# Seven column blocks of one projection multiplied with seven block products in place of eight, in a trunk layer in fp32

## The chip, the cores and the metric

The kernel runs on one core of one Trainium2 chip. The metric is the device time of one execution in microseconds (us). Everything that the text touches is fp32. The engines are named as the profile names them: PE is the matrix engine (TensorE), PEld its weight loads, DVE is VectorE, ACT is ScalarE, POOL is GpSimd, SP is the engine that issues most of the weight loads; SPq, ACTq and so on are their instruction queues.

## The reference, cut to what matters

The layer takes 384 tokens (128 of context and 256 latent ones) of width 1024. The change is in one product, `h @ w_in`, and only in some of its columns: the output gate of the linear attention (`g_out`, 512 columns) and the two branch gates (`gate_br_conv` and `gate_br_gla`, 1024 columns each).

```
h = rmsnorm(x, norm1_w) * (1 + sc1) + sh1
(u_in, gate_b, gate_c, q, k, v, g_out, lr_f, lr_b,
 gate_br_conv, gate_br_gla) = jnp.split(h @ w_in, points, axis=-1)
y_conv = gate_b * conv3_rows(gate_c * u_in, conv_w, conv_b, rows, row_len)
y_gla, s_f, s_b = gla_mixer(q, k, v, g_out, lr_f, lr_b, ...)      # ends in  o * silu(g_out)
merged = (sigmoid(gate_br_conv) * (y_conv @ w_br_conv)
          + sigmoid(gate_br_gla) * (y_gla @ w_br_gla))
x = x + g1 * (merged @ w_out)
h2 = rmsnorm(x, norm2_w) * (1 + sc2) + sh2
x = x + g2 * moe(h2, ...)                                          # 64 experts, top 8, and a shared one
```

The modulation rows `sh1 ... g2` are `silu(cond) @ w_mod + b_mod`, with `w_mod` of 1024 x 6144.

## The kernel before, in words

The normalised input lies transposed in `hT`: 128 partitions, 8 blocks of features (k), 384 tokens. A column tile of the projection is 128 columns of `w_in`: `project_part` (L1904) runs 8 matmuls for it, one for each k, each with 128 x 128 weights and 384 moving columns (L1910), into one of the 8 PSUM banks. The profile shows each fp32 matmul as two records. In the names of the code "u", "gc", "gb", "k", "q", "v", "go", "gbc" and "gbg" are the pieces of `w_in`: "go" is `g_out` (4 column tiles), "gbc" and "gbg" are the branch gates (8 tiles each).

**Units.** Weights come in units of 1 MB: two column tiles of `w_in` (so "go" has units 0 and 1, "gbg" units 0 to 3), or one k of a third of `w_mod` ("mod"). The units stand in one written order, `plan_units` (L103), and go through a ring of 5 places. SP loads a unit into the place of the unit five earlier in the order (L1561), in order, and waits before it until that older unit has been used: for a unit of `w_in` until PE has finished its last tile, for a "mod" unit until DVE has added it. Around the change the order is v0, v1, mod 1.4, go0, mod 1.5, go1, mod 1.6, gbc0, mod 1.7, gbc1, gbc2, gbc3, mod 2.0, mod 2.1, gbg0, mod 2.2, mod 2.3, gbg1, mod 2.4, mod 2.5, gbg2, mod 2.6, mod 2.7, gbg3, and then the weights of the branch projections. ("mod 2.3" is k = 3 of the last third of `w_mod`.)

**Modulation.** DVE multiplies each "mod" unit by the activated condition and adds it, in `add_modulation` (L463: two scalar_tensor_tensor of 128 x 2048, one for each condition). PE then sums the result over the partitions in `sum_modulation` (L1900), which waits until all 8 units of that third have been added: `sum_modulation(1)` stands behind the attention's transposes (L2014), `sum_modulation(2)` between gbg tiles 5 and 6.

**Order of the work.** It is written out by hand for each engine. PE: u, gc, gb, k, q, v, then the four "go" tiles, eight groups of three transposes ("kt", L2014), `sum_modulation(1)`, the attention with gbc tiles 0 to 3 between its pieces, gbc 4 and 5, the transposes of the attention's output ("oT", L2025), gbc 6 and 7, gbg 0 to 5, `sum_modulation(2)`, gbg 6 and 7, the branch projections ("mc", "mg", L2082), the output projection (L2096), routing and experts. A job of PE takes a bank in the turn that `plan_jobs` and `bank_of` set and waits (`start`) until the job before in that bank has been drained. ACT drains the gate tiles with Silu (L1754) or Sigmoid (L1762). POOL has nothing to do between its constants at the start and the expert stage. DVE works through its own list: after gate factors and the sums of `mod 1`, the attention's masks and states, the output's norm, and then mod 2.1 to 2.7 in one row.

## Time and profile before

| | us |
|---|---|
| median of 3 runs (955.33 to 955.88) | 955.38 |
| the profiled execution, whole | 957.51 |
| its span, first to last instruction | 955.8 |
| PE busy (95% of the span) | 910.9 |
| DVE busy (45%) | 426.2 |
| ACT busy (20%) | 187.8 |
| POOL busy (10%) | 94.7 |
| POOL: 34 indirect stores of expert rows (L597), 30 indirect loads (L591), mean of one | 1.01, 1.06 |

The mean granted clock of TensorE was 0.992. The profiled execution is 2.1 us longer than the median. The busy share of PE is an average: the projection (up to 288 us from the span's start), the branch and output projections (to 385 us) and the expert stage (to about 907 us) each have a limit of their own, and so a stage is read by itself. In the page's row of 40 slices the DMA engines are at 3 to 7 tenths in most slices up to 400 us and at 9 in all behind it.

### The profile page before, as it was taken

To read this page: it belongs to the slowest core of one execution; us is meant where nothing else is said; L and a number is where in the kernel's file an instruction comes from. 1 tells how busy PE (TensorE), PEld (TensorE's weight loads), DVE (VectorE), ACT (ScalarE), POOL (GpSimd) and SP (SyncE) were. 2 spreads that over 40 slices of the span, in tenths; PEclk is the share of its full clock that TensorE was granted. 3 is DMA by queue.
4 is the path that set the end of the run, shared out by engine and by line. 5 is a ranking of instruction groups with operands and counts; after the bars stand their busy time and mean duration, and the time that the engine had idled before them with its cause. 6 is when DMAs were issued, how large, how long until landed. Compare 5 with 4: busy or idle time off the path is not lost.

```text
span 955.8 us, 13246 instructions
## 1 busy us (share of the span) xinstructions
PE 910.9 (95%) x4997; PEld 487.7 (51%) x4997; DVE 426.2 (45%) x770; ACT 187.8 (20%) x309; POOL 94.7 (10%) x198
## 2 busy tenths in 40 slices
PE   5999999999999999999999999989999989899995
PEld 2455567676555687544444444434445453454432
DVE  4129966534762346463333333323233323323267
ACT  3150601212100013112212212111111211211111
POOL 2000000000000000202112111111111201111100
PEclk9999999999999999999999999999999999999998
DMA  9998453625677356799999999999999999999995
GB/s 344 355 404 327 132 201 142 229 89 177 237 292 269 125 245 240 279 395 374 420 419 420 420 420 420 420 421 421 419 421 419 421 423 418 423 420 420 420 418 220
DMA packets 85034, 322.04 MB, mean 337 GB/s; under 512 B 10084, under 2 KB 38936, under 8 KB 56040
## 3 DMA queue, kind: packets, MB, share of 16 engines
q1 hardware_dynamic: 70368, 289.43, 76.3%
q0 software_dynamic: 9216, 22.22, 6.0%
q10 hardware_dynamic: 5384, 9.51, 2.8%
q8 instruction: 42, 0.69, 0.3%
q14 instruction: 24, 0.20, 0.1%
HBM read 298.36 MB, written 34.11 MB: 348 GB/s over the span
## 4 chain that ended last, share of the span: by engine, by line
PE 88%; DMA 5%; DVE 2%; issue 2%; ACT 2%; SPq 1%; DVEq 0%; POOLq 0%
PE bank L624 25%; PE bank L1910 22%; PE bank L653 13%; PE bank L2096 4%; PE bank L2082 4%; PE bank L610 3%; DMA arena<-expert_rows 3%; PE bank L2002 2%; PE bank L2124 2%; PE bank L604 2%; PE bank L577 2%; PE bank L1886 1%; PE bank L642 1%; PE bank L2194 1%; ACT arena L635 1%
## 5 line engine op out<-in xcount | busy, mean ns | idle before, releaser
L624 PE MATMUL bank<-arena 128*32 128x512 f32 (+2 forms) x1568 | 256.8, 598 | 9.0 <-issue 9.0
L1910 PE MATMUL bank<-arena 128*128 128x384 f32 x640 | 211.6, 490 | 2.4 <-ACT arena L1697 2.4
L624 PEld LDWEIGHTS bank<-arena 128*32 128x32 f32 (+2 forms) x1568 | 89.8, 123 | 171.7 <-issue 171.6
L1910 PEld LDWEIGHTS bank<-arena 128*128 128x128 f32 x640 | 121.1, 191 | 86.5 <-issue 7.0
L653 PE MATMUL bank<-arena 128*32 128x512 f32 (+2 forms) x784 | 131.5, 596 | 4.9 <-issue 4.2
L653 PEld LDWEIGHTS bank<-arena 128*32 128x32 f32 (+2 forms) x784 | 43.1, 122 | 69.8 <-issue 69.1
L658 DVE SCALAR_TENSOR_TENSOR arena<-bank,arena 128x512 f32<-128x512 f32 x36 | 27.0, 751 | 106.5 <-PE bank L653 106.3
L666 ACT ACTIVATE arena<-arena 128x1024 f32<-128x1024 f32 x36 | 41.3, 1148 | 163.1 <-DVE arena L662 159.3
L463 DVE SCALAR_TENSOR_TENSOR arena<-arena 128x2048 f32<-128x2048 f32 x28 | 64.6, 2348 | 18.8 <-DMA arena<-in_w_mod_dram 17.7
L638 DVE TENSOR_TENSOR arena<-arena,bank 128x256 f32<-128x256 f32 x36 | 21.9, 607 | 85.6 <-ACT arena L635 85.6
L570 DVE TENSOR_TENSOR arena<-arena 128x288 f32<-128x288 f32 (+3 forms) x64 | 22.0, 380 | 82.1 <-POOL arena L741 41.1
L597 POOL DMA_INDIRECT expert_rows<-arena x34 | 34.4, 1010 | 230.7 <-DVE arena L662 230.7
L635 ACT ACTIVATE arena<-bank 128x256 f32<-128x256 f32 x36 | 22.2, 618 | 170.4 <-PE bank L624 170.4
L591 POOL DMA_INDIRECT arena<-h_rows,arena x30 | 31.9, 1063 | 182.3 <-issue 152.4
L615 DVE COPY arena<-bank 128x512 f32<-128x512 f32 x36 | 24.9, 692 | 52.4 <-PE bank L610 30.1
L669 DVE SCALAR_TENSOR_TENSOR arena<-arena 128x1024 f32<-128x1024 f32 x36 | 46.1, 1279 | 3.5 <-ACT arena L666 3.5
L2096 PE MATMUL bank<-arena 128*128 128x256 f32 x192 | 42.0, 379 | 0.0
L577 PEld LDWEIGHTS bank<-arena 128*64 128x64 f32 (+3 forms) x432 | 28.8, 137 | 25.8 <-issue 25.4
L2082 PE MATMUL bank<-arena 128*128 128x384 f32 x128 | 41.4, 486 | 0.0
L2096 PEld LDWEIGHTS bank<-arena 128*128 128x128 f32 x192 | 36.3, 190 | 5.1
L720 POOL IOTA arena<- 128x96 int32 (+3 forms) x4 | 1.4, 357 | 378.1 <-DVEq L1430 377.9
L604 PE MATMUL bank<-arena 128*128 128x128 f32 x240 | 37.4, 279 | 0.0
(262 smaller groups left out, 794.7 us busy)
## 6 DMA issues: line engine op xcount, KB each, us to landing
arena<-in_w_up_e_dram SPq DMA_DIRECT2D x64, 1024.0 KB, 29.2
arena<-in_w_down_e_dram SPq DMA_DIRECT2D x64, 1024.0 KB, 29.2
arena<-in_w_gate_e_dram SPq DMA_DIRECT2D x64, 1024.0 KB, 27.0
arena<-in_w_mod_dram SPq DMA_DIRECT2D x24, 1024.0 KB, 7.5
arena<-in_w_in_dram SPq DMA_DIRECT2D x22, 1024.0 KB, 7.7
expert_rows<-arena SPq DMA_DIRECT2D x6, 2048.0 KB, 22.4
arena<-expert_rows SPq DMA_DIRECT2D x12, 1024.0 KB, 24.9
arena<-in_w_out_dram SPq DMA_DIRECT2D x4, 1024.0 KB, 5.4
```

The costliest lines, as they stand in the source:

```text
L463: ins = eng.scalar_tensor_tensor(out=mod_acc[:, s, :], in0=unit_view(u), scalar=scond[:, s, k:k + 1], in1=mod_acc[:, s, :], op0=ALU.mult, ...
L577: ins = pe.matmul(banks[7][o:o + w, 0:4], onehot[b][:, t, o:o + w], qv[:, b % 2, s, t, :], start=(t == 0), stop=(t == NT - 1))
L591: pool.indirect_dma_start(out=x_g[b], out_offset=None, in_=h2_dram, in_offset=bass.IndirectOffsetOnAxis(ap=rows_i[:, g, 0:1], axis=0), bou ...
L597: pool.indirect_dma_start(out=rows_dram, out_offset=bass.IndirectOffsetOnAxis(ap=rows_i[:, g, 1:2], axis=0), in_=y_e[b], in_offset=None, b ...
L604: ins = pe.transpose(banks[k // 4][:, P * (k % 4):P * (k % 4) + P], x_g[b][:, P * k:P * k + P], ident)
L624: ins = pe.matmul(bank[off:off + width, :], x_T[:, k, off:off + width], w[:, :, k, :], start=(k == 0), stop=(k == KT - 1))
L653: ins = pe.matmul(banks[5 + i][off:off + width, :], actT_e[:, P * k + off:P * k + off + width], w[:, k, 512 * i:512 * i + 512], start=(k = ...
L666: return act.activation(gate_rows, g2_rows[:, 0, :], ACT.Copy, scale=of_seq[:, 0, g:g + 1])
L669: return dve.scalar_tensor_tensor(out=gate_rows, in0=g2_rows[:, 1, :], scalar=of_seq[:, 1, g:g + 1], in1=gate_rows, op0=ALU.mult, op1=ALU.add)
L1910: ins = pe.matmul(ps[:, 0:TOK], w[:, k, P * (n % 2):P * (n % 2) + P], hT[:, k, :], start=(k == 0), stop=(k == KT - 1))
L2082: ins = pe.matmul(ps[:, 0:TOK], w[:, k, P * (n % 4):P * (n % 4) + P], y[:, k, :], start=(k == 0), stop=(k == CT - 1))
L2096: ins = pe.matmul(ps[:, 256 * j:256 * j + 256], merged[:, k, P * t:P * t + P], w[:, k, :], start=(k == 0 and (j == 0 or len(merged_tiles) ...
```

## The change

Seven units (`SEVEN`: go0, go1, gbc3, gbg0, gbg1, gbg2, gbg3) are no longer multiplied by `project_part`. The unit's weights (1024 x 256) and the tokens (1024 x 384) are cut into 2 x 2 blocks: weights W11, W12, W21, W22 of 512 x 128, tokens X11, X12, X21, X22 of 512 x 192. Eight block products become seven, after Strassen in Winograd's form, with sums of blocks on both sides:

- POOL builds the four token sums T1 to T4 once (128 x 768 each), when `hT` is done, and for each of the seven units three weight sums S1, S2, S4 and, over W21 in its own place in the ring, W11 - W21 (four tensor_tensor of 128 x 512). It waits for the unit to land; PE waits for the sums.
- PE runs 28 matmuls with 192 moving columns for each unit (`seven_products`), into three banks. Two of the products are needed in more than one sum. PSUM can't be copied by PE, so ACT copies three partial results ("snaps") to SBUF while PE goes on, and PE waits for the copy before it accumulates further into the same bank.
- DVE puts the four output blocks together from banks and snaps (`join_parts`: five tensor_tensor of 128 x 192) and only then frees the three banks. These joins stand at written places between its additions of mod units.
- ACT applies Silu or Sigmoid to the first block from the bank and to the other three blocks (128 x 576) in place, after the join.

The banks are numbered anew (one job more for each unit). Five semaphores are merged into one counter (`step_done`), two into `consts`. SBUF for the sums and snaps: the arena grows by 3072 words in each partition (12 KB), and the scratch for the descriptors of GpSimd's DMAs is set to 4096 bytes in each partition, by an argument that was not given before.

```diff
+HALF = TOK // 2
+SEVEN = [("go", 0), ("go", 1), ("gbc", 3), ("gbg", 0), ("gbg", 1), ("gbg", 2), ("gbg", 3)]
...
+def with_seven(jobs):
+    for m, (name, i) in enumerate(SEVEN):
+        jobs.insert(jobs.index((name, 2 * i + 1)), ("seven", m))
...
-        SIZE = 53200
+        SIZE = 53200 + 3072
...
+            def join_parts(m, dst):
+                a, b, c = seven_jobs(m)
+                one, six, five = snaps[m % 2]
+                for job in (a, b, c):
+                    full(dve, job)
+                dve.wait_ge(S["snap_taken"], 4 * m + 4)
+                link(dve.tensor_tensor(six, one, six, ALU.add))
+                link(dve.tensor_tensor(one, bank(b)[:, 0:HALF], one, ALU.add))
+                dve.tensor_tensor(dst[:, c[1], 0:HALF], one, bank(a)[:, HALF:TOK], ALU.subtract)
+                dve.tensor_tensor(dst[:, c[1], HALF:TOK], one, five, ALU.add)
+                link(dve.tensor_tensor(dst[:, a[1], HALF:TOK], bank(c)[:, 0:HALF], six, ALU.add))
+                for job in (a, b, c):
+                    dve.sem_inc(bank_free[bank_of[job]], 1)
+                dve.sem_inc(S["parts_done"], 1)
...
             for k in range(4, KT):
                 add_modulation(dve, 1, k, link)
+                if k == 5:
+                    join_parts(0, y_gla)
+            join_parts(1, y_gla)
             mod_bias(1)
...
             for k in range(1, KT):
                 add_modulation(dve, 2, k, link)
+                if k in (2, 3, 5):
+                    join_parts((2, 3, 5).index(k) + 2, g_conv if k == 2 else g_gla)
             mod_bias(2)
+            join_parts(5, g_gla)
...
+            join_parts(6, g_gla)
...
+            link(pool.tensor_tensor(t1, x12, x11, ALU.subtract))
+            link(pool.tensor_tensor(t3, x22, x12, ALU.subtract))
+            link(pool.tensor_tensor(t2, x22, t1, ALU.subtract))
+            link(pool.tensor_tensor(t4, t2, x21, ALU.subtract))
+            pool.sem_inc(S["sums_ready"], 1)
+            for m, u in enumerate(SEVEN):
+                unit_arrived(pool, u)
+                if m >= 2:
+                    pool.wait_ge(S["fac_ready"], 8)
+                if m >= 4:
+                    full(pool, seven_jobs(m - 2)[2])
+                w11, w12, w21, w22 = quarters(u)
+                s1, s2, s4 = sums_of(m)
+                link(pool.tensor_tensor(s1, w21, w22, ALU.add))
+                pool.tensor_tensor(w21, w11, w21, ALU.subtract)
+                link(pool.tensor_tensor(s2, s1, w11, ALU.subtract))
+                link(pool.tensor_tensor(s4, w12, s2, ALU.subtract))
+                pool.sem_inc(S["sums_ready"], 1)
             pool_experts(pool, link)
...
+            def take_snaps(m, dst, func):
+                a, b, c = seven_jobs(m)
+                if m >= 2:
+                    act.wait_ge(S["parts_done"], m - 1)
+                for n, job in enumerate((a, b, c)):
+                    act.wait_ge(S["product_done"], 3 * m + n + 1)
+                    act.activation(snaps[m % 2][n], bank(job)[:, 0:HALF], ACT.Copy).then_inc(S["snap_taken"], 1)
+                full(act, a)
+                act.activation(dst[:, a[1], 0:HALF], bank(a)[:, 0:HALF], func).then_inc(S["snap_taken"], 1)
...
+            take_snaps(0, y_gla, ACT.Silu)
+            take_snaps(1, y_gla, ACT.Silu)
+            rest_of_gate(0, y_gla, ACT.Silu)
...
+            def seven_products(m):
+                a, b, c = seven_jobs(m)
+                out_a, out_b, out_c = start(a), start(b), start(c)
...
+                arrived(SEVEN[m])
+                pe.wait_ge(S["sums_ready"], m + 2)
...
+                product(out_a[:, second], w22, t4, True)
+                product(out_a[:, first], w11, hT[:, 0:4, first], False).then_inc(S["product_done"], 1)
+                product(out_b[:, first], s2, t2, True).then_inc(S["product_done"], 1)
+                product(out_c[:, first], s1, t1, True).then_inc(S["product_done"], 1)
+                pe.wait_ge(S["snap_taken"], 4 * m + 2)
+                finish(product(out_b[:, first], w21, t3, False), b)
+                finish(product(out_a[:, first], w12, hT[:, 4:8, first], False), a)
+                pe.wait_ge(S["snap_taken"], 4 * m + 3)
+                finish(product(out_c[:, first], s4, hT[:, 4:8, second], False), c)
...
-            project("go", CT)
+            seven_products(0)
+            seven_products(1)
...
-            project("gbc", KT, NH + 2)
-            project("gbg", 6)
+            for m in range(2, 6):
+                seven_products(m)
             sum_modulation(2)
-            project("gbg", KT, 6)
-
-            pe.wait_ge(S["gla_ready"], 1)
+            seven_products(6)
+
+            step(pe, "gla_ready")
...
-    nc = _bacc.Bacc("TRN2", target_bir_lowering=False, num_devices=1)
+    nc = _bacc.Bacc("TRN2", target_bir_lowering=False, num_devices=1, dynamic_dma_scratch_size=4096)
```

Each of the four matmuls of a `product` is over one k of its half.

The order on PE from the "v" tiles to the attention, before ("bank" is a PSUM bank, "arena" the SBUF; L1910 projects, L2014 is "kt", L1900 `sum_modulation`):

```order
L2002 MATMUL bank<-arena 128x256 x48
L1910 MATMUL bank<-arena 128x384 x32
L2014 MATMUL bank<-arena 128x128 x24
L1900 MATMUL bank<-arena 2x512 x8
L2033 MATMUL bank<-arena 128x128 x6
```

and after (L2041 is the `product` of `seven_products`, L2150 is "kt", L2009 `sum_modulation`):

```order
L2137 MATMUL bank<-arena 128x256 x48
L2041 MATMUL bank<-arena 128x192 x56
L2150 MATMUL bank<-arena 128x128 x24
L2009 MATMUL bank<-arena 2x512 x8
L2169 MATMUL bank<-arena 128x128 x6
```

The place of everything is kept; 32 matmuls of 384 columns have become 56 of 192.

The order on DVE from the norm of the attention's output to the branch projections, before (L461 and L463 are `add_modulation`, L1302 multiplies the transposed output by its gate, L1120 and L1315 close the third part of the modulation, L1322 begins the merge):

```order
L1295 TENSOR_TENSOR arena<-arena 128x1536
L461 TENSOR_SCALAR arena<-arena 128x2048 x2
L1302 SCALAR_TENSOR_TENSOR arena<-bank,arena 128x384 x4
L463 SCALAR_TENSOR_TENSOR arena<-arena 128x2048 x14
L1120 TENSOR_TENSOR arena<-bank,arena 2x512 x4
L1315 SCALAR_TENSOR_TENSOR arena<-arena 2x512 x2
L1322 TENSOR_TENSOR arena<-bank,arena 128x384
```

and the first part of it after (L501 and L503 are `add_modulation`, L1360 the gate, L1273 to L1277 `join_parts`):

```order
L501 TENSOR_SCALAR arena<-arena 128x2048 x2
L1360 SCALAR_TENSOR_TENSOR arena<-bank,arena 128x384 x4
L503 SCALAR_TENSOR_TENSOR arena<-arena 128x2048 x4
L1273 TENSOR_TENSOR arena<-arena 128x192
L1274 TENSOR_TENSOR arena<-bank,arena 128x192
L1275 TENSOR_TENSOR arena<-arena,bank 128x192
L1276 TENSOR_TENSOR arena<-arena 128x192
L1277 TENSOR_TENSOR arena<-bank,arena 128x192
L503 SCALAR_TENSOR_TENSOR arena<-arena 128x2048 x2
```

The row of 14 additions is cut: a join (2) stands behind the first four, a join (3) behind two more, then four additions (mod 2.4 and 2.5), join 4, and the last four (mod 2.6 and 2.7); joins 5 and 6 follow behind the additions that L1120 and L1315 were before, one behind each. Before, DVE waited for PE at none of these places.

## Rows read from the trace of the kernel before

**Rows 1.** The page's part on the chain that ended last, by line.
```profile
PE bank L624 25%; PE bank L1910 22%; PE bank L653 13%; PE bank L2096 4%; PE bank L2082 4%; PE bank L610 3%; DMA arena<-expert_rows 3%; PE bank L2002 2%; PE bank L2124 2%; PE bank L604 2%; PE bank L577 2%; PE bank L1886 1%; PE bank L642 1%; PE bank L2194 1%; ACT arena L635 1%
```
**Rows 2.** The chain in order of time, go tiles: start us, us, what.
```profile
160.71 20.65 PE bank L1910 x64
182.51 2.03 ACT arena L1758 x5
184.59 1.90 PE bank L1900 x16
```
**Rows 3.** The same chain, the later gate tiles and single later pieces.
```profile
234.22 41.28 PE bank L1910 x128
275.51 1.90 PE bank L1900 x16
277.40 10.52 PE bank L1910 x32
287.92 41.28 PE bank L2082 x128
329.20 27.63 PE bank L2096 x128
...
671.26 2.68 PE bank L610 x24
```
**Rows 4.** ACT, timeline: a go tile drained (start us, us, ... [idle before]).
```profile
165.91 0.49 ACT L1754 ACTIVATE arena<-bank 128x384 f32<-128x384 f32 x1 [3.26 <-PE bank L1910]
```
**Rows 5.** POOL, groups by form: the operations that read SBUF, by width.
```profile
L776 POOL CAST arena<-arena 128x384 f32<-128x384 int32 x1 | 0.6, 565 | 0.1
L722 POOL CAST arena<-arena 128x128 f32<-128x128 int32 x1 | 0.3, 289 | 0.1
```
**Rows 6.** SP's queue, timeline: mod 2.2 and 2.3, then mod 2.4 and 2.5.
```profile
232.94 11.96 SPq L1561 DMA_DIRECT2D arena<-in_w_mod_dram  x2
...
245.42 9.80 SPq L1561 DMA_DIRECT2D arena<-in_w_mod_dram  x2
```
**Rows 7.** Single loads of L1561: issue (ns, start us), landing: go1, gbg1, gbg2.
```profile
L1561 SPq DMA_DIRECT2D arena<-in_w_in_dram x1: 368/368/368, 160.7 to 160.7; - x1
DMA to landing us min/median/max: 5.3/5.3/5.3
...
L1561 SPq DMA_DIRECT2D arena<-in_w_in_dram x1: 434/434/434, 244.9 to 244.9; - x1
DMA to landing us min/median/max: 8.9/8.9/8.9
...
L1561 SPq DMA_DIRECT2D arena<-in_w_in_dram x1: 434/434/434, 255.3 to 255.3; - x1
DMA to landing us min/median/max: 7.4/7.4/7.4
```
**Rows 8.** DVE, timeline: additions of mod units, and two short tensor_tensor.
```profile
106.27 0.29 DVE L1242 TENSOR_TENSOR arena<-arena 128x128 f32<-128x128 f32 x1
106.48 0.42 DVE L1243 TENSOR_TENSOR arena<-arena 128x256 f32<-128x256 f32 x1
...
168.63 4.62 DVE L463 SCALAR_TENSOR_TENSOR arena<-arena 128x2048 f32<-128x2048 f32 x2 [8.62 <-DMA arena<-in_w_mod_dram]
...
249.52 4.62 DVE L463 SCALAR_TENSOR_TENSOR arena<-arena 128x2048 f32<-128x2048 f32 x2 [4.15 <-DMA arena<-in_w_mod_dram]
...
256.31 18.90 DVE L463 SCALAR_TENSOR_TENSOR arena<-arena 128x2048 f32<-128x2048 f32 x8 [2.18 <-DMA arena<-in_w_mod_dram]
```
**Rows 9.** PE, timeline, and three windows (fields, then PEclk, DMA share, GB/s).
```profile
25.38 7.09 PE L1910 MATMUL bank<-arena 128*128 128x384 f32 x16 [2.43 <-ACT arena L1697]
...
25.40:27.00 1.60, 1.60 (x4) 0.86 (x5) 0.00 (x0) 0.00 (x0) 0.00 (x0) 0.66 1.05 385
27.00:28.00 1.00, 1.00 (x3) 0.59 (x2) 0.00 (x0) 0.00 (x0) 0.00 (x0) 0.50 1.06 389
...
30.00:31.00 1.00, 1.00 (x4) 0.57 (x3) 0.00 (x0) 0.00 (x0) 0.00 (x0) 1.00 1.05 387
```

More of the change, by code:

```diff
@@ L168, in program @@
     for n, j in enumerate(in_turn):
-        bank_of[j] = n % 6 if n < early else (n - early) % 8 if n < late else late_bank[n - late]
+        bank_of[j] = n % 6 if n < early else (n - early + 4) % 8 if n < late else late_bank[n - late]
     for j, b in zip(at_start, start_banks, strict=True):
@@ L293, in program @@
         folded = at(a_x + 3 * D + 512, 512)
+        sum_places = [(a_rms, a_rms + 512, a_rms + 1024), (a_sq, a_s0 + 1024, a_s0 + 1536),
+                      (a_mix, a_mix + 512, a_mix + 1024), (a_mix + 1536, a_mix + 2048, a_mix + 2560)]
+        weight_sums = [[at(a, 4, P) for a in place] for place in sum_places]
         def score_tile(n):
@@ L323, in program @@
         wr = at(a_z, KT, NE)
-        restart = at(take(TOK), TOK)
+        a_restart = take(TOK)
+        restart = at(a_restart, TOK)
+        snap_places = [a_g2 + D + HALF * n for n in range(5)] + [a_restart]
+        snaps = [[at(a, HALF) for a in snap_places[3 * n:3 * n + 3]] for n in range(2)]
         mask = [arena[:, a:a + TOK // 4].bitcast(U8) for a in (take(TOK // 4), take(TOK // 4))]
@@ L367, in program @@
         deal = {128: at(a_before, 128), 96: at(a_before + 128, 96), 64: at(a_iota, 64), 32: at(a_iota + 64, 32)}
+        a_t = take(4 * 4 * HALF)
+        token_sums = [at(a_t + 4 * HALF * n, 4, HALF) for n in range(4)]
         ident = at(take(P), P)
@@ L453, in unit_arrived, with step, seven_jobs, quarters @@
             eng.wait_ge(unit_in[n % UNITS], 16 * (n // UNITS + 1))
+        def step(eng, name):
+            eng.wait_ge(S["step_done"], STEPS.index(name) + 1)
+        def seven_jobs(m):
+            name, i = SEVEN[m]
+            return (name, 2 * i), ("seven", m), (name, 2 * i + 1)
+        def quarters(u):
+            w = unit_view(u)
+            return [w[:, a:a + 4, b:b + P] for b in (0, P) for a in (0, 4)]
+        def sums_of(m):
+            return weight_sums[m if m < 2 else 2 + m % 2]
+        def gate_ready(eng, name, n):
+            if (name, n // 2) in SEVEN:
+                eng.wait_ge(S["gate_done"], SEVEN.index((name, n // 2)) + 1)
+            else:
+                drained(eng, (name, n))
         def add_modulation(eng, g, k, link):
@@ L1751, in _ @@
                 free(act.activation(v_sb[:, t, :], bank(("v", t))[:, :], ACT.Copy), ("v", t))
-            for n in range(CT):
-                full(act, ("go", n))
-                free(act.activation(y_gla[:, n, :], bank(("go", n))[:, 0:TOK], ACT.Silu), ("go", n))
+            take_snaps(0, y_gla, ACT.Silu)
+            take_snaps(1, y_gla, ACT.Silu)
+            rest_of_gate(0, y_gla, ACT.Silu)
             for d in range(2):
@@ L1799, in spread_mods @@
                         .then_inc(S["mods_spread"], 16)
-            gate("gbg", g_gla, [KT - 1])
+            rest_of_gate(6, g_gla, ACT.Sigmoid)
             spread_mods()
@@ L1918, in project, with product @@
                     project_part(name, n, 0, KT)
+            def seven_products(m):
+                a, b, c = seven_jobs(m)
+                out_a, out_b, out_c = start(a), start(b), start(c)
+                first, second = slice(0, HALF), slice(HALF, TOK)
+                w11, w12, w21, w22 = quarters(SEVEN[m])
+                s1, s2, s4 = sums_of(m)
+                t1, t2, t3, t4 = token_sums
+                arrived(SEVEN[m])
+                pe.wait_ge(S["sums_ready"], m + 2)
+                def product(out, w, x, fresh):
+                    for k in range(4):
+                        ins = pe.matmul(out, w[:, k, :], x[:, k, :], start=(fresh and k == 0), stop=(k == 3),
+                                        skip_group_check=True)
+                    return ins
+                product(out_a[:, second], w22, t4, True)
[7 more added lines that the diff above has]
+                finish(product(out_c[:, first], s4, hT[:, 4:8, second], False), c)
             def transpose_in(k):
```

63 lines of the change are left out of this document (41 added, 22 removed).

## The prediction, on record before the changed kernel ran

> **What bounds the kernel now.** I read the chain of waits by line first: PE stands on it nearly everywhere, the projection line L1910 with 22% and the expert lines L624 and L653 with 38% together; DVE and ACT hardly appear [rows 1]. So a microsecond taken from PE's matmuls counts, unless something else is late behind it. Then I read the same chain in order of time around the seven units. The four go tiles are one unbroken piece of 20.65 us, followed by the kt transposes, which wait on ACT for a moment, and `sum_modulation(1)` at 184.59 [rows 2]. The later gate tiles are another unbroken piece: 8 tiles in 41.28 us from 234.22, `sum_modulation(2)` at 275.51, two tiles, and the branch projections begin at 287.92 [rows 3]. PE waits for nothing in them. I then looked for what PE would wait for if it had less to do: the loads in SP's queue, DVE's additions, and the price of an operation on POOL.
>
> **What PE saves.** 128 records of 384 columns in 41.28 us are 322.5 ns each; 128 records of 256 columns in 27.63 us are 215.9 ns; 24 of 128 columns in 2.68 us are 111.7 ns [rows 3]. 192 columns lie midway between the last two: 163.8 ns. A unit had 32 records, 10.32 us; it gets 28 matmuls, 56 records, 9.17 us. That is 1.15 us for each unit, 8.0 us for seven: 2.3 in the go stage, 5.7 in the later one. One product less in eight would be 1.29; the shorter matmuls give 0.14 of it back.
>
> **Snaps: nothing.** PE needs the copy of bank b after the four matmuls of the next product, 8 x 0.164 = 1.31 us after b is complete. ACT drains 384 columns in 0.49 us [rows 4], and 192 can't take longer. The copy of c has two products of time. ACT is otherwise idle there. If it were late, every us would go to PE.
>
> **The sums on POOL.** The trace has no operation of POOL with two inputs. The nearest are conversions with one input: 289 ns for 128 columns, 565 ns for 384 [rows 5], so 1.08 ns a column and 0.15 us fixed. 512 columns are 0.70 us by that (the low bound), and 0.15 + 2 x 0.55 = 1.25 us if two inputs are read one after the other. I take the second, since both inputs have to pass, and 0.2 us for the semaphores between the four: 5.2 us a unit (low bound 4 x 0.70 + 0.2 = 3.0). The high bound is in the rival on DVE. The Trainium skill (GPSIMD Engine Reference, Elementwise, side-by-side cycle accounting) has a two-input add of 2048 fp32 columns at 4497 ns and calls it a floor of the read port; by it 512 columns would be an estimated 1.1 us and the four sums 4.7 us, 0.5 less than mine. Token sums: 4 x (0.15 + 2 x 0.83) = 7.2 us near 55 us, needed at 160: hidden.
>
> **What the sums wait for.** They can't begin before the unit has landed, and from gbg1 on a unit is asked for late. In the order of units SP loads mod 2.3 into the place of gbc3, and only then gbg1. Before, gbc3's last tile ended at 234.22 + 10.32 = 244.5; SP's pair begun at 232.94 ended its second issue with 11.96 us [rows 6], gbg1 was issued at 244.9 and landed 8.9 us later, at 253.8, just ahead of PE's need at 254.9; gbg2 took 7.4 us [rows 7]. That margin of 1.1 us is all there is, and the sums need 5.2. Now, counted from 234.22:
> - unit gbc3 (its sums long made) ends at 243.4; gbg1 is issued 0.4 later, at 243.8, and lands at 252.7;
> - gbg0 (asked for a whole gate unit earlier, so its sums are made too) ends at 252.56; the sums of gbg1 are there at 257.9. PE waits 5.3 us;
> - such a wait has a second price. After PE had been idle for 2.43 us at 23 us, the granted clock was 0.66, then 0.50, and 1.00 again from 30 us; 16 records took 7.09 us instead of 5.16 [rows 9], 1.9 us more: the engine had fallen from 2.4 to 1.2 GHz. I add 1.9. gbg1 ends at 269.0;
> - gbg2 was issued at the end of gbg0 and is summed by 265.6: no wait. It ends at 278.2.
>
> **DVE.** Join 4 can't start before gbg1 is complete, 269.0. The join's five operations: a tensor_tensor of 128 columns is 0.29 us and of 256 columns 0.42 [rows 8], so 0.36 for 192, with the semaphores between them 2.0 us. Behind it stand mod 2.6 and 2.7, 4.62 us each [rows 8]: 269.0 + 2.0 + 9.24 = 280.2. Before, the last eight additions ran in one row and ended at 275.2, when PE wanted them. `sum_modulation(2)`, queued behind gbg2, therefore waits 2.0 us, and ends at 282.1. gbg3, issued at 269.4 and landed by 276.8, is summed by 282.0. The last unit runs from 282.1 to 291.3. The clock may fall in this gap too; it is a little shorter than the one in the row, so I count half, 1.0. Branch projections: 292.3 against 287.92, **4.4 us later**, although PE has 5.7 us less to do. Joins 5 and 6 come in the first 5 us of the branch projections, where before DVE had waited for PE: hidden; PE has all the other banks.
>
> **The go stage.** go0, which was loaded while the v tiles were multiplied, runs from 160.71 to 169.9. go1 is issued at 160.7 when v is done and lands at 166.0 [rows 7]; its sums are there at 171.2, PE waits 1.4 us, and the unit ends at 180.4. DVE waits for join 0 until 169.9, where it used to start mod 1.6 at 168.63 [rows 8], adds mod 1.6 and 1.7 until 181.1, joins unit 1 until 183.1. The first five kt groups have free banks; the last three take those of go1 and wait for that join. Their nine transposes of 128 columns take 9 x 0.112 = 1.0 us, until 184.1; ACT drains the one in `sum_modulation(1)`'s bank in 0.49 [rows 4], and that starts at 184.7 against 184.59: **0.1 later**. The 2.3 us are gone into DVE's list.
>
> **The rest.** Loads of the later stages are released by PE's or DVE's progress, so I let the shift pass whole to the end. The smaller descriptor scratch: no cost, as the indirect DMAs are issued singly. The clock at full rate, merged semaphores and new banks: nothing.
>
> **Sum.** 4.4 + 0.1 = +4.5 us. The profiled execution took 957.51, so 962.0 by its own time; it lies 2.1 above the median of the runs, and against 955.38 the forecast is 959.9.
>
> **Rival 1: POOL and DVE hold each other up.** Both work in SBUF at the same time from 252.7 on, and no row before shows such a pair. If an operation with two SBUF inputs on one engine has to let the other's finish first, the sums of gbg1 stand behind parts of DVE's instructions of 2.31 us: two of the four lose some 1.6 us each, PE's wait becomes 8.6 us, gbg2's sums come 3.0 late as POOL's operations alternate with mod 2.4 and 2.5, and the four operations of 1.25 that DVE has to let pass make its list 1.4 later at `sum_modulation(2)`. That adds 3.3 + 3.0 + 1.4 = 7.7: +12.2, 967.6. The Trainium skill (SBUF — State Buffer, Who interferes with whom) states just this: a DVE instruction with two SBUF inputs and a GpSimd one that reads SBUF exclude each other for the whole instruction. For it: the two would often meet, as DVE added for 23.5 of the 25.7 us from 249.52 to 275.21 [rows 8]. Against it: nothing that the trace can show.
>
> **Rival 2, the other side: the sums are nearly hidden.** With POOL at the low bound, 3.0 us, and gbg1 landing in 7.4 us as gbg2 did, PE waits for gbg1 until 254.2 or 1.7 us, and too little for the clock to fall. gbg1 ends at 263.4, DVE's list at 274.6, so `sum_modulation(2)` waits 2.0 and the branch projections begin at 285.7, 2.2 us earlier: 953.2. The point from which it decides: with DVE's 2.0 us, the 5.7 us saved pay for 3.7 of waiting, which is a landing and sums of 12.5 us together after the issue, if the clock stays. By the values above they are 14.1.
>
> **Rival 3: the shift doesn't arrive.** From 400 us on the DMA engines are at 9 tenths. If the stream of expert weights sets the pace there and not PE, a few us later or earlier are taken up: within 0.2% of before, 955.4 to 957. Against it, the chain lies on PE in that stage [rows 1].
>
> **Rival 4: the scratch.** POOL issues 34 scatters and 30 gathers. If each scatter had to wait for room in a smaller scratch, and DVE for the scatter before it writes the next rows, a us of excess in each would be +34. I see no reason for it in the rows: they come one by one, with PE's whole pass through an expert pair between them.
>
> **Chances.** Forecast 0.42 (its own range 957 to 963), rival 1 0.21, rival 2 0.25, rival 3 0.10, rival 4 0.02. The runs of this kernel can't tell less than 0.2%, 1.9 us, from no change. Faster is rival 2; within the bound are rival 3 and the lower edge of the forecast; slower the rest. The range 952.0 to 968.0 leaves out a part of rival 1, rival 4 and a rival 2 with still earlier landings.
>
> **What would show it.** Right: records of L2041 at 164 ns; PE idle before L2041 at about 252 for 4 to 6 us, released by POOL, and clock below 1.00 behind it; a wait of some 2 us before L2009; POOL's tensor_tensor at 1.1 to 1.3 us; kt's last groups released by DVE's L1277. Rival 1: POOL's operations, or DVE's additions, longer or spaced when both run. Wrong: gbg1 landing so early that PE isn't idle, or L2041 records far from 164 ns.

## The result, and the profile after

| | before | changed |
|---|---|---|
| median in the same batch, us | 955.63 (955.33 to 956.93) | 972.1 (971.24 to 974.12) |
| ratio, 95% interval | 1 | 1.0169 (1.0156 to 1.0181) |
| profiled execution: span, us | 955.8 | 972.4 |
| mean granted clock | 0.992 | 0.987 |
| PE busy, us | 910.9 | 906.7 |

The kernel became slower by 16.5 us, against 4.5 forecast, and the time lies outside the range of 952 to 968. PE does 4 us less and ends 17 us later. A second batch gave 1.0172 (1.0158 to 1.0185).

The page's row of the seven products (line, engine, operation, form, count; busy us, mean ns of one; idle us before it and its releaser) shows both at once:

```profile
L2041 PE MATMUL bank<-arena 128*128 128x192 f32 x392 | 68.5, 339 | 12.2 <-POOLq L1741 9.2
```

L1741 is POOL's signal that the weight sums are there. The chain of the changed kernel in the late gate stage (start us, us, what) answers to [rows 3]:

```profile
234.81 9.12 PE bank L2041 x56
...
251.67 2.73 POOL arena L1737
...
257.15 3.20 POOL arena L1740
...
260.53 11.45 PE bank L2041 x56
...
272.19 0.37 DVE arena L1273
...
274.29 4.62 DVE arena L503 x2
...
279.05 5.63 DVE arena L503 x2
...
284.97 3.36 PE bank L2009 x16
...
291.24 11.02 PE bank L2041 x56
302.26 10.00 PE bank L2218 x31
```

Where [rows 3] has PE alone from 234.22 to 287.92, the chain now goes through POOL, PE, DVE and PE again. I call the stretch from gbc3's unit to the branch projections (L2218) the late stage: **53.70 us before, 67.45 after, 13.75 more**. The go stage ahead of it ends 0.6 later (234.81 against 234.22) and what follows it takes 2.3 longer (670.1 against 667.9 us). 13.75 + 0.6 + 2.3 is the difference of the spans, 16.6.

The late stage in parts, each read from this chain: five units of 9.12 us for ten tiles save 51.80 - 45.60 = 6.2. PE's idle stretches are 7.5 before gbg1, 3.9 before `sum_modulation(2)` (L2009), 2.9 before the last unit. The clock takes 2.3 (11.45 for 9.12), 1.5 (3.36 for 1.90) and 1.9 (11.02 for 9.12). 7.5 + 3.9 + 2.9 + 2.3 + 1.5 + 1.9 - 6.2 = 13.8.

The clock itself, in windows cut at these places (stretch, its length; busy us of PE, PEld, DVE, ACT, POOL with counts; granted clock, DMA share, GB/s):

```profile
235.00:253.90 18.90, 18.02 (x111) 17.72 (x110) 17.12 (x15) 3.21 (x9) 2.23 (x1) 1.00 0.58 214
253.90:260.50 6.60, 0.00 (x0) 0.00 (x0) 6.10 (x7) 0.00 (x0) 6.28 (x4) 0.81 1.03 354
260.50:265.00 4.50, 4.47 (x15) 4.50 (x16) 4.35 (x2) 0.00 (x0) 4.10 (x2) 0.52 0.45 184
265.00:281.00 16.00, 16.00 (x99) 15.77 (x98) 12.20 (x10) 3.79 (x10) 7.60 (x4) 1.00 0.51 179
```

In the second row PE does nothing while DVE and POOL are busy nearly all the time. In the third it has work again and runs at the low level, 1.2 GHz (granted clock 0.52 over 4.5 us); in the fourth it is at 2.4 GHz.

POOL's own list in that time (start us, us, engine, line, operation; idle before it):

```profile
251.67 2.72 POOL L1737 TENSOR_TENSOR arena<-arena 128x512 f32<-128x512 f32 x1 [16.72 <-DMA arena<-in_w_in_dram]
254.47 1.26 POOL L1738 TENSOR_TENSOR arena<-arena 128x512 f32<-128x512 f32 x1
255.70 1.37 POOL L1739 TENSOR_TENSOR arena<-arena 128x512 f32<-128x512 f32 x1
257.15 3.19 POOL L1740 TENSOR_TENSOR arena<-arena 128x512 f32<-128x512 f32 x1
260.82 2.79 POOL L1737 TENSOR_TENSOR arena<-arena 128x512 f32<-128x512 f32 x1 [0.48 <-DMA arena<-in_w_in_dram]
263.68 3.20 POOL L1738 TENSOR_TENSOR arena<-arena 128x512 f32<-128x512 f32 x1
266.85 3.31 POOL L1739 TENSOR_TENSOR arena<-arena 128x512 f32<-128x512 f32 x1
270.24 1.26 POOL L1740 TENSOR_TENSOR arena<-arena 128x512 f32<-128x512 f32 x1
```

One operation is 1.26 us, the forecast's 1.25, or some 3.2. The long ones stand where DVE adds mod units, and the short ones at 254.47, 255.70 and 270.24 stand where DVE is at join 3 or waits for join 4. DVE's additions beside them, two units each (9.24 us alone, [rows 8]; start us, us, engine, line, operation; idle before them):

```profile
256.64 12.39 DVE L503 SCALAR_TENSOR_TENSOR arena<-arena 128x2048 f32<-128x2048 f32 x4 [0.43 <-DVE arena L1277]
...
274.29 10.38 DVE L503 SCALAR_TENSOR_TENSOR arena<-arena 128x2048 f32<-128x2048 f32 x4 [0.43 <-DVE arena L1277]
```

DVE's additions of the last third of `w_mod`, grouped, before and after:

```profile
L463 DVE SCALAR_TENSOR_TENSOR arena<-arena 128x2048 f32<-128x2048 f32 x14 | 32.3, 2348 | 7.1 <-DMA arena<-in_w_mod_dram 6.3
...
L461 DVE TENSOR_SCALAR arena<-arena 128x2048 f32<-128x2048 f32 x2 | 2.5, 1282 | 0.1
```
```profile
L503 DVE SCALAR_TENSOR_TENSOR arena<-arena 128x2048 f32<-128x2048 f32 x14 | 36.3, 2635 | 2.1 <-DVE arena L1277 0.9 <-DMA arena<-in_w_mod_dram 0.7
L501 DVE TENSOR_SCALAR arena<-arena 128x2048 f32<-128x2048 f32 x2 | 4.3, 2172 | 0.1
```

4 us longer for the same 14 additions, and two of L501 (L461 before) take 4.3 us beside the sums of gbg0, in place of 2.5. Two theories stood to be told apart. **Theory A**: POOL and DVE exclude each other (rival 1 of the prediction), and most of the loss follows from it. **Theory B**: POOL only waits for memory behind the loads, which run at full share in the second window, and the loss is the landing, DVE's list and the banks.

### The profile page after: what moved, and what is told of

It reads as the page before. It is cut to its first block, busy times and chain, and to the rows that moved or that the text cites. A ratio compares the mean times of both kernels' runs of the same rounds, so it can differ in the third digit from the quotient of the medians.

```text
span 972.4 us, 13732 instructions
## 1 busy us (share of the span) xinstructions
PE 906.7 (93%) x5165; PEld 511.8 (53%) x5165; DVE 448.7 (46%) x805; ACT 194.5 (20%) x330; POOL 156.3 (16%) x230
## 4 chain that ended last, share of the span: by engine, by line
PE 83%; DMA 6%; DVE 5%; issue 3%; ACT 1%; POOL 1%; SPq 1%; DVEq 0%; POOLq 0%
PE bank L664 24%; PE bank L2019 14%; PE bank L693 13%; PE bank L2232 4%; PE bank L2218 4%; PE bank L2041 4%; PE bank L650 3%; DMA arena<-expert_rows 3%; PE bank L2137 2%; PE bank L2260 2%; PE bank L644 2%; DVE arena L503 2%; PE bank L617 2%; PE bank L1995 1%; PE bank L682 1%
## 5 line engine op out<-in xcount | busy, mean ns | idle before, releaser
L2019 PE MATMUL bank<-arena 128*128 128x384 f32 x416 | 138.7, 492 | 2.4 <-ACT arena L1800 2.4
L2019 PEld LDWEIGHTS bank<-arena 128*128 128x128 f32 x416 | 78.8, 192 | 56.6 <-issue 5.9
L2041 PE MATMUL bank<-arena 128*128 128x192 f32 x392 | 68.5, 339 | 12.2 <-POOLq L1741 9.2
L2041 PEld LDWEIGHTS bank<-arena 128*128 128x128 f32 x392 | 67.4, 199 | 14.5 <-issue 14.5
L706 ACT ACTIVATE arena<-arena 128x1024 f32<-128x1024 f32 x36 | 41.3, 1148 | 162.9 <-DVE arena L702 159.2
L503 DVE SCALAR_TENSOR_TENSOR arena<-arena 128x2048 f32<-128x2048 f32 x28 | 69.6, 2527 | 3.1 <-DVE arena L1277 1.3
L1737 POOL TENSOR_TENSOR arena<-arena 128x512 f32<-128x512 f32 x7 | 13.8, 1966 | 184.7 <-DMA arena<-in_w_in_dram 184.7
L2218 PE MATMUL bank<-arena 128*128 128x384 f32 x128 | 41.4, 486 | 0.0
```

What stands on the lines that cost most here:

```text
L503: ins = eng.scalar_tensor_tensor(out=mod_acc[:, s, :], in0=unit_view(u), scalar=scond[:, s, k:k + 1], in1=mod_acc[:, s, :], op0=ALU.mult, ...
L706: return act.activation(gate_rows, g2_rows[:, 0, :], ACT.Copy, scale=of_seq[:, 0, g:g + 1])
L2019: ins = pe.matmul(ps[:, 0:TOK], w[:, k, P * (n % 2):P * (n % 2) + P], hT[:, k, :], start=(k == 0), stop=(k == KT - 1))
L2041: ins = pe.matmul(out, w[:, k, :], x[:, k, :], start=(fresh and k == 0), stop=(k == 3), skip_group_check=True)
L2218: ins = pe.matmul(ps[:, 0:TOK], w[:, k, P * (n % 4):P * (n % 4) + P], y[:, k, :], start=(k == 0), stop=(k == CT - 1))
```

## The experiments

Stage lengths are of the profiled execution: the late stage, and "rest" from its end to the end of the span. Both are read from each run's chain. The rest varied from 666.6 to 670.1 us among all kernels without pattern, so for effects of 2 us the stage says more than the whole time. e2_no_sums, e3_no_adds and e7_no_sums_late leave out work that the result needs, so their routing, and with it their rest, can differ.

| kernel | late stage | rest | ratio to before, 95% interval |
|---|---|---|---|
| before | 53.7 | 667.9 | 1 |
| changed | 67.4 | 670.1 | 1.0169 (1.0156 to 1.0181) |
| e1_bank | 62.4 | 667.3 | 1.0148 (1.0123 to 1.0173) |
| e2_no_sums | 59.9 | 668.5 | 1.0105 (1.0088 to 1.0122) |
| e3_no_adds | 59.0 | 668.7 | 1.0082 (1.0065 to 1.0099) |
| e4_scratch | 53.6 | 666.6 | 1.000 (0.9991 to 1.001) |
| e5_four | 52.8 | 667.7 | 0.9999 (0.999 to 1.0008) |
| e7_no_sums_late | 47.9 | 669.2 | 0.9978 (0.9969 to 0.9987) |
| e8_three | 51.0 | 666.9 | 0.9969 (0.9958 to 0.9979) |
| e9_mod_late | 53.4 | 667.8 | 1.0001 (0.9991 to 1.001) |
| e10_joins_behind | 66.7 | 668.1 | 1.0211 (1.0197 to 1.0225) |
| e11_same | 68.8 | 668.4 | 1.0172 (1.0158 to 1.0185) |

### e1_bank: another bank for sum_modulation(2)

```diff
-    for j, after in zip(apart, (("kt", 1, 1), ("gbg", 1))):
+    for j, after in zip(apart, (("kt", 1, 1), ("seven", 4))):
```

In the changed kernel `sum_modulation(2)` takes the bank of gbg tile 1. With the banks numbered anew that is bank 7, and the last unit's middle product is next in bank 7: PE can't start the unit until DVE's L1160 has read the sum.

> The changed kernel with one edit: the bank of sum_modulation(2) is bank 1 (free since join 4) in place of bank 7, which the last of the seven units needs for its second output. Theory (a missed wait): in the changed kernel PE stood idle for 2.9 us before the last unit, from the end of sum_modulation(2) at 288.3 until DVE had drained bank 7 at 291.2. With another bank that wait goes: the last unit begins at about 288.4, when POOL's sums for it are ready (they ended at 288.37), the branch projections at about 299.4 and not 302.3: 972.1 - 2.8 = 969.3. Rival (the wait is for DVE's additions or the sums anyway): less than 1 us.

Measured: the wait before the last unit is gone, and with it the fall of the clock behind it. The chain:

```profile
281.82 2.71 POOL arena L1737
...
289.10 1.28 POOL arena L1740
290.57 9.34 PE bank L2041 x56
```

The stage is 5.1 shorter, more than the wait of 2.9 alone: the last unit takes 9.34 and not 11.02 us, and another 0.5 us comes from the earlier part of the stage (gbg1 takes 10.73 and not 11.45 us). What holds the last unit now is the sums of gbg3, for 0.25 us. The whole time fell by only 2.2 (969.86 against 972.1 in another batch; the intervals of the two ratios overlap). The profiled execution had a longer go stage: its late stage began at 237.53 (below, e11_same).

### e2_no_sums and e3_no_adds: POOL without DVE, DVE without POOL

e2_no_sums replaces the four operations and the wait for the unit, so that PE never waits for a sum. POOL fills the places once instead; its twelve operations for that run from 144.65 to 173.2 us, beside DVE, so this kernel shows the late stage without the sums and not the go stage.

```diff
-                unit_arrived(pool, u)
+                if m < 2:
+                    unit_arrived(pool, ("go", 0))
...
-                link(pool.tensor_tensor(s1, w21, w22, ALU.add))
...
+                if m < 4:
+                    for s in sums_of(m):
+                        link(pool.tensor_tensor(s, hT[:, 0:4, 0:P], hT[:, 4:8, 0:P], ALU.add))
```

> The changed kernel without the weight sums of the seven units: POOL fills the places of the sums once, early, from the tokens, and then only signals, so PE waits for the unit alone; W21 stays as loaded. The gates are then not the reference's, and so routing can differ: the start of the branch projections tells more than the whole time. Theory (the loss is POOL's sums, late and long, and what follows from them): the 7.5 us wait before gbg1 goes, DVE's additions take 4.6 us a unit again, and the branch projections begin between 286 and 290 (302.3 with the sums, 287.9 before): join 4 and two units of additions still hold sum_modulation(2) for some 2 us, and the shared bank the last unit for 2.9. Time 955 to 959. Rival (PE's own part costs more than counted: snaps, joins, banks): the branch projections still begin after 293, time over 962.

e3_no_adds keeps POOL's sums and leaves out DVE's additions beside them:

```diff
+            if g == 2 and k >= 3:
+                eng.sem_inc(S["mod_unit_added"], 1)
...
+                return
```

> The changed kernel without DVE's additions of mod 2.3 to 2.7: DVE waits for these units and signals, but adds nothing; the modulation rows and with them routing are not the reference's. Theory (the two engines exclude each other while both read two SBUF inputs): each of POOL's operations for gbg1, gbg2 and gbg3 takes 1.26 us, where beside the additions it took 2.7 to 3.3; PE waits 3.5 to 4 us for gbg1 and not 7.5, and the branch projections begin at 291 (302.3 with the additions). Time about 961. Rival (POOL is slow there because the loads write SBUF at 320 to 350 GB/s at that time): POOL's operations stay at 2.7 to 3.3, the wait for gbg1 stays over 7 us; only the wait before sum_modulation(2) (3.9 us) goes: 968.

Measured, e3_no_adds: POOL's list for gbg1, with the loads going on (318 GB/s from 251.9 to 257.5 us):

```profile
252.05 1.27 POOL L1742 TENSOR_TENSOR arena<-arena 128x512 f32<-128x512 f32 x1 [16.71 <-DMA arena<-in_w_in_dram]
253.40 1.26 POOL L1743 TENSOR_TENSOR arena<-arena 128x512 f32<-128x512 f32 x1
254.62 1.38 POOL L1744 TENSOR_TENSOR arena<-arena 128x512 f32<-128x512 f32 x1
256.08 1.27 POOL L1745 TENSOR_TENSOR arena<-arena 128x512 f32<-128x512 f32 x1
```

All twelve operations of the late units are 1.26 to 1.38 us, where they were 1.26 to 3.31. PE's wait for gbg1 is 4.1 in place of 7.5, so of those 7.5 us 4.1 are landing and sums, and 3.4 are DVE. Theory B's memory is out. The windows of the changed kernel say the same: POOL's 254.47 and 255.70 took 1.26 and 1.37 us at 354 GB/s, and its 263.68 and 266.85 took 3.20 and 3.31 at 184 and 179 GB/s. A's mechanism holds. The branch projections began at 294.17 where 291 was expected: the clock took 2.7 us behind the wait for gbg1, and the bank's wait of 3.0 with 1.8 of clock behind it stayed.

But A's size does not hold. In e2_no_sums PE ran without a stop through gbc3, gbg0, gbg1 and gbg2, 9.1 us each as counted, and then still waited 5.9 for `sum_modulation(2)` and 3.0 for the bank. I had expected a stage of 52 to 56 us and got 59.9. The start of the branch projections (296.83) and the time (966.56) are those that I had put down for the rival there, that PE's own part costs more than counted; PE's units don't, the joins on DVE do. DVE's list (the additions and join 4):

```profile
257.79 9.37 DVE L503 SCALAR_TENSOR_TENSOR arena<-arena 128x2048 f32<-128x2048 f32 x4 [0.43 <-DVE arena L1277]
267.49 0.36 DVE L1273 TENSOR_TENSOR arena<-arena 128x192 f32<-128x192 f32 x1 [0.32 <-ACT arena L1771]
...
269.60 9.37 DVE L503 SCALAR_TENSOR_TENSOR arena<-arena 128x2048 f32<-128x2048 f32 x4 [0.43 <-DVE arena L1277]
```

From the end of the additions at 267.16 to the start of the next at 269.60 a join costs DVE 2.44 us, and it starts as soon as DVE comes to it: gbg1 is long complete. The list ends at 279.0, 42.0 us into the stage that began at 236.93. Before, it ended 41.0 us into the stage, when PE wanted it (41.3); now PE wants it after 36.4. The list can't start at will either: mod 2.3 is loaded into the place of gbc3 when PE has finished that unit, 9.1 us into the stage, and the additions of mod 2.3 begin at 250.75. **DVE's list is a second bound**: it doesn't follow PE when PE gets faster, even with free sums.

### e4_scratch: the kernel before with the smaller descriptor scratch

```diff
-    nc = _bacc.Bacc("TRN2", target_bir_lowering=False, num_devices=1)
+    nc = _bacc.Bacc("TRN2", target_bir_lowering=False, num_devices=1, dynamic_dma_scratch_size=4096)
```

> The kernel before with one edit: the scratch for the descriptors of GpSimd's DMAs is 4096 bytes in each partition. Theory: no change, ratio 1.000 within 0.2%, indirect DMAs at 1.01 and 1.06 us. Rival (the smaller scratch holds up the expert stage, where the changed kernel's profile was a further 2.5 us later): 2 us slower, 957.6.

Measured: 956.27 against 956.72 in the batch, no difference. Rival 4 is out.

### e7_no_sums_late: what is left when all waits are taken away

e2_no_sums with `sum_modulation(2)` behind the last unit, joins 5 and 6 ahead of `mod_bias(2)`, and a bank that isn't needed again before the third job of "mc":

```diff
-            sum_modulation(2)
             seven_products(6)
+            sum_modulation(2)
...
-            mod_bias(2)
             join_parts(5, g_gla)
+            join_parts(6, g_gla)
+            mod_bias(2)
```

> POOL makes no weight sums (the seven units' results are not the reference's, and routing can differ), sum_modulation(2) stands behind the last unit in a bank of its own turn (that of gbg tile 5), joins 5 and 6 ahead of what DVE does with its result. Theory (with sums free, DVE's list ends 42 us behind the start of the late gate stage, which is earlier than PE's five units): no wait on PE at all, five units of 9.1 and 1.9 for sum_modulation(2), stage 47.5 us against 53.7 of before, 59.9 without sums and with the old place; whole time 954.3, which is 2.4 below before, the 5.7 saved less what the go stage loses. Rival (DVE's list, or a further wait nobody has named, still holds PE): stage 50 or more. Second rival (time saved in the stage is absorbed later): stage 47.5 and a time of 956.7 or more.

Measured: no wait for sums, modulation or bank. The end of the chain in this stage:

```profile
264.28 18.44 PE bank L2037 x112
282.72 1.83 PE bank L2005 x16
284.55 15.68 PE bank L2214 x48
```

47.9 us, 5.8 less than before, so the 6 us of the products are real in the stage. 2.4 of them are spent in the go stage (the late stage began at 236.61 against 234.22), which leaves 3.4. The median fell by 1.7 (955.06 against 956.8, ratio 0.9978; 954.3 was expected), so this kernel, with a routing of its own, passes on about half. Rival 3, that a shift is absorbed later, goes by the two kernels that compute the reference's result: the changed kernel is 14.3 us late at the branch projections and 16.5 at the end, and e8_three below is 3.8 early there and 3.1 at the end.

### e5_four and e8_three: units only where there is room, and e9_mod_late as their control

e5_four drops gbg1 to gbg3 from `SEVEN`; e8_three also drops go1 and puts `sum_modulation(2)` behind gbg tile 7, in tile 6's bank; e9_mod_late does the latter alone to the kernel before.

```diff
-SEVEN = [("go", 0), ("go", 1), ("gbc", 3), ("gbg", 0), ("gbg", 1), ("gbg", 2), ("gbg", 3)]
+SEVEN = [("go", 0), ("gbc", 3), ("gbg", 0)]
...
+            project("go", CT, 2)
...
-            for m in range(2, 6):
-                seven_products(m)
-            sum_modulation(2)
-            seven_products(6)
+            seven_products(1)
+            seven_products(2)
+            project("gbg", KT, 2)
+            sum_modulation(2)
```

> Four units by the seven products (go0, go1, gbc3, gbg0); gbg1, gbg2 and gbg3 by project_part as before, so that POOL makes no sums for them and no join stands between mod 2.4 and mod 2.7. Theory (the loss is made of three things in the late gate stage: PE waits for landing and sums of gbg1, DVE's list with joins 4 to 6 ends later, and sum_modulation(2)'s bank): all three go, the stage from gbc3 to the branch projections takes 2 x 9.1 + 3 x 10.3 + 1.9 = 51.0 us, or up to 53 if DVE's eight additions behind join 3 end after PE's second plain unit (53.7 before, 67.45 in the changed kernel). The whole: 955.5 to 957.5 against 956.7 of before, since the go stage keeps its +0.4 to +2.4. Rival (the scheme costs something everywhere, such as a lower clock or a later stream of expert weights): 960 or more with a late stage of 51 to 53.

> Seven products only for go0, gbc3 and gbg0, where the unit has landed long before and POOL and DVE have room; go1 and gbg1 to gbg3 by project_part; sum_modulation(2) behind the last tile in gbg tile 6's bank. Theory: no wait is added, each unit saves 1.15 us: the late stage takes 2 x 9.1 + 3 x 10.3 + 1.9 = 51.1 us (53.7 before), the go stage 1.15 less, the whole 953.2 at 956.7 of before. Rival (DVE's join 0 between the additions of mod 1.5 and 1.6, and POOL's sums of 1.2 us or more on top, make sum_modulation(1) late also here): 955 to 957, with PE idle before it. Second rival (a shift isn't passed on to the end): stage lengths as in the theory and a time of 956 to 957.

> The kernel before with sum_modulation(2) behind gbg tile 7 in place of between tiles 5 and 6, in tile 6's bank: the control for the kernel with three units. Theory: PE didn't wait there before, so nothing moves: late stage 53.7 us, 956.7, ratio 1.000 within 0.001. Rival (the place itself is worth something, because the bias rows end nearer to the branch projections or the clock rises): 0.5 us or more either way.

Measured: e5_four 956.51 against 956.8, no difference: 2.4 us saved by two units, 1.5 of them lost waiting for DVE's list before `sum_modulation(2)`, and 1.4 lost in the go stage. e9_mod_late: no difference, so the place alone is worth nothing measurable. e8_three: 953.71 (952.63 to 954.23) against 956.8, **ratio 0.9969 (0.9958 to 0.9979), 3.1 us faster**, where 3.5 were expected. Its chain:

```profile
233.16 18.20 PE bank L2037 x112
251.36 30.96 PE bank L2015 x96
282.32 1.83 PE bank L2005 x16
284.15 16.00 PE bank L2214 x49
```

PE alone again, as in [rows 3], and 51.0 us long where 51.1 were expected. POOL's sums of gbg0 meet DVE's L501 here too and take 1.57, 2.13, 2.24 and 1.27 us, but the unit had landed 16 us before PE came to it, so nobody waits. The go stage kept little of its 1.2: from the first matmul of go0 to the late stage it is 73.2 us, 73.5 before. `sum_modulation(1)` starts 1.0 earlier by that count, and then POOL's sums of gbc3 meet DVE's work for the attention. One operation there, L1333 (two inputs in SBUF), took 0.56 us before (L1275) and 1.29 now, and PE waits 0.57 for it:

```profile
188.84 1.29 DVE L1333 SCALAR_TENSOR_TENSOR arena<-arena 128x384 f32<-128x384 f32 x1
```

### e10_joins_behind and e11_same: the go stage

The changed kernel's go stage has its own waits. PE waits 1.7 us for the sums of go1. DVE waits for join 0 until PE's first unit is done; its chain from there (changed kernel):

```profile
170.09 0.37 DVE arena L1273
...
172.31 4.63 DVE arena L503 x2
...
177.08 4.63 DVE arena L503 x2
...
182.11 0.37 DVE arena L1273
```

and kt's last groups wait for join 1, 1.3 us. I took DVE for the bound, and let it add on without a stop:

```diff
                 add_modulation(dve, 1, k, link)
-                if k == 5:
-                    join_parts(0, y_gla)
+            join_parts(0, y_gla)
             join_parts(1, y_gla)
```

> The changed kernel with one edit: join 0 stands behind the additions of mod 1.6 and 1.7 together with join 1, in place of between them and those of 1.4 and 1.5. Theory (in the go stage DVE is what PE waits for: join 0 stops its additions until PE's first unit is done and POOL's sum can make its first operation 1.2 us in place of 0.37): the additions run on without a stop and end about 178, both joins end by 182.8, kt's last groups start 1 to 1.5 us earlier than 184.2, with no fall of the clock in kt and sum_modulation(1); the late gate stage starts at 233.7 against 234.8 to 237.4; whole time 1 to 3 below the changed kernel of the same batch. Rival (kt's wait is set by PE's own end and the snaps, and DVE's joins in a row take as long as before): start of the late stage within 0.5 of the changed kernel's.

> The changed kernel once more, in the batch of the kernel with joins 0 and 1 behind the additions, to tell what of the go stage's length is spread between executions: theory (whether POOL's sum meets join 0's first operation is chance, and the wait before kt's last groups then is 1.3 or 2.4 us, the latter with a lower clock behind it): 969 to 973 us, late gate stage 67 us, its start anywhere from 234.8 to 237.4.

Measured: a miss with the sign reversed. e10_joins_behind took 977.26 against 973.44 of the changed kernel in the same batch, and its late stage began at 240.70. The last of POOL's four sums of go1, first in it, then in the changed kernel:

```profile
...
167.00 1.26 POOL L1737 TENSOR_TENSOR arena<-arena 128x512 f32<-128x512 f32 x1
168.22 3.38 POOL L1738 TENSOR_TENSOR arena<-arena 128x512 f32<-128x512 f32 x1
171.68 3.02 POOL L1739 TENSOR_TENSOR arena<-arena 128x512 f32<-128x512 f32 x1
```
```profile
...
168.80 1.27 POOL L1739 TENSOR_TENSOR arena<-arena 128x512 f32<-128x512 f32 x1
170.15 1.26 POOL L1740 TENSOR_TENSOR arena<-arena 128x512 f32<-128x512 f32 x1
```

The stop at join 0 had kept DVE out of POOL's way. Without it the additions started at 168.12, two of POOL's operations took over 3 us, and PE waited 5.5 for go1 and ran the unit in 12.11 us (clock 0.50 in its first 5 us). I had priced DVE's side of the edit and not POOL's, after having seen the exclusion in the late stage.

e11_same began its late stage at 237.33 and e1_bank at 237.53, with the code of the changed kernel in the go stage, where the first profile has 234.81. In both, POOL's last sum of go1 met join 0's first operation (1.08 and 1.18 us in place of 0.37), kt's last groups waited 2.4 in place of 1.3 us, and kt's last nine records and the sum behind them took 2.18 and 2.48 us (1.20 and 1.83 in the first profile): the granted clock from 183.9 to 188.6 us is 0.64 in e11_same. Another 0.9 us of the difference is PE waiting for DVE's L1333, which met POOL's sums of gbc3 there (1.63 us; in the first profile 0.71, and no wait). So with one code the go stage ended 0.6, 3.1 or 3.3 us late. That a few tenths of a microsecond of timing decide it is how I read it; e5_four had the same meeting and the same wait of 2.4, its clock stayed at 1.00, and it ended 1.4 late.

The late stage of e11_same is 68.8 us, where I had expected 67: its three waits are those of the first profile, but the clock behind them took 3.2, 0.5 and 3.3 us.

## Why the prediction was wrong, step by step

- **PE's products, right.** 56 records took 9.11 to 9.12 us, forecast 9.17; snaps cost nothing; POOL's operation alone 1.26, forecast 1.25. The saving of 5.7 in the late stage was 6.2.
- **What the sums wait for: right in kind, too small by 2.2.** The wait before gbg1 was forecast at 5.3 and measured at 7.5. Without DVE's additions it is 4.1 (e3_no_adds): gbg1 landed 16.8 us into the stage, 1.7 earlier than the 18.5 of the forecast, and the sums with the signals around them took some 0.4 longer. The other 3.4 are the exclusion, which the forecast left to rival 1. Rival 1 had 3.3 for this wait, and for DVE's list 1.4, where the additions of mod 2.6 and 2.7 took 10.4 in place of 9.24. Its third term, 3.0 for gbg2's sums, came to nothing: they took 10.7 us, but ended at 271.50, 0.5 before PE was done with gbg1. Its 967.6 misses the bank and the price of the clock as the forecast does.
- **DVE's wait: the right limit, 3.9 in place of 2.0, and a second limit not seen.** As forecast, join 4 waits for gbg1 and `sum_modulation(2)` for the additions behind it (chain above). But the join with what lies around it takes 2.3 and not 2.0, the four additions 10.4 and not 9.24, because one pair meets POOL, and the signals 0.3. Behind this limit stands the list's own length: with the sums free PE still waits 5.9 (e2_no_sums), since joins of 2.4 each fill a list that had 7.1 us idle in it and none behind 256 us [rows 8]. Rival 2 (953.2) put DVE's end at 274.6, which is 40.4 into the stage, and PE's need at 38.3; with free sums they are 42.0 and 36.4. Its landing came true (7.3 us), its sums of 3.0 us did not (5.3 without DVE). Even with no sums at all and without the bank's 2.9 and 1.9 the stage would be 55.1, still over 53.7, so a chance of 0.25 for it was too much.
- **"Merged semaphores and new banks: nothing", the step that was missed.** The bank of `sum_modulation(2)` is shared with the last unit. 2.9 us of wait, and 1.9 of clock behind it; e1_bank took both away (5.1 in the stage). With the part that came from earlier in the stage left out, e1_bank's gain is 4.4. It could be read from the change: the banks are numbered by a formula over the list of jobs, which the change had lengthened by seven and shifted by four, while the exception that gives `sum_modulation(2)` the bank of gbg tile 1 was kept. Before, that bank was next needed by the second branch projection tile, behind gbg 6, gbg 7 and a tile more.
- **The clock, too small.** The forecast has 1.9 + 1.0; the profiled execution has 2.3, 1.5 and 1.9 in the late stage, one for each wait, even that of 2.9 us, and e11_same 3.2, 0.5 and 3.3.
- **The go stage: 0.1 forecast, 0.6 to 3.3 measured.** The forecast had no exclusion there, neither at join 0 nor between the sums of gbc3 and L1333, and no fall of the clock.
- **The scratch, and the shift that arrives: right** (e4_scratch; the changed kernel and e8_three).

In numbers for the late stage: forecast +4.4, measured +13.8; the exclusion at gbg1 less the earlier landing 2.2, the longer wait for DVE 1.9, the bank 2.9, the clock 0.4 + 0.5 + 1.9, and -0.5 for products: 9.3 of the 9.4. The rest of the miss in the spans is 0.5 in the go stage and 2.3 behind the late stage in that execution. What made these 2.3 I didn't settle; in e11_same, the same kernel, that part took 1.7 less.

The Trainium skill (SBUF — State Buffer, Who interferes with whom) states that a DVE instruction with two SBUF inputs contends with a GpSimd one that reads SBUF, and calls the ports that they share an exclusive lock. The runs agree in the main: a POOL operation of 1.26 became 3.2, which is short of 1.26 + 2.31 by 0.4, and DVE's pair of additions became 5.63 for 4.62, a gain of 1.0 and not of the whole 1.26. I had cited this section and given its result 0.21.

## What to carry to other kernels

Before work is given to an idle engine, ask whether it meets another engine's operations on the same memory, and price both directions: the added work waits, and what it meets waits. Then write the lists of all engines around the place, each with its own end and no help from the others' waits; what is saved on the engine that bounds is lost as soon as any other list ends later than the new, earlier need. Do such a change first where the data has landed long before: three units of seven gave 0.3%, all seven lost 1.7%.

## What the runs showed of the hardware

- A tensor_tensor of 128 x 512 fp32 on POOL, both inputs in SBUF: 1.26 us alone, up to 3.4 beside scalar_tensor_tensor of 128 x 2048 on DVE; of 128 x 768, 1.8 us. DVE's tensor_scalar of 128 x 2048, with one tensor as its input, suffered as well, 2.5 to 4.3 us for two, and so did a join operation of 0.37 us, up to 1.3, and a scalar_tensor_tensor of 128 x 384, from 0.56 to 1.6.
- PE's clock fell behind waits of 2.9, 3.9 and 7.5 us, at 0.5 to 3.3 us each. Behind one of 2.4 before kt it fell in e1_bank and e11_same and stayed in e5_four; what tells them apart, no row shows.
- Starting DVE's additions earlier (e10_joins_behind) made the whole slower by 3.8 us: a wait on one engine can be what keeps another one fast.
